# Early first gathers, a shorter first lag, and a combine in which TensorE adds two of four planes

## The reference, cut to what matters

```python
# first block, its last step
top_vals, top_idx = lax.top_k(logits, TOP_K)          # 4 of 32 experts for each token
weights = jax.nn.softmax(top_vals, axis=-1)
gu = xblk @ w_gu[e] + b_gu[e]                         # for the tokens of each expert
act = (up + 1.0) * gate * jax.nn.sigmoid(SWIGLU_ALPHA * gate)
y = act @ w_down[e] + b_down[e]                       # summed per token with weights
h = h + g2 * y
x = rmsnorm(h, final_norm_w)
# second block, its first step
h = rms_norm(x, norm_mix_pre[l])
proj = h @ w_in[l]
```

## Time and profile before

| | |
|---|---|
| median of 3 runs | 2189.33 us (2187.8 to 2194.87) |
| the profiled execution's own time | 2191.0 us |
| its span, first to last instruction | 2189.2 us |
| TensorE / VectorE / ScalarE / GpSimd busy | 1967.4 / 933.3 / 375.2 / 375.4 us |
| bytes moved, mean rate | 557.00 MB, 254 GB/s |
| mean granted TensorE clock | 0.948 |

### The profile page before, as it was taken

The page is one execution under the profiler, slowest core; times in us unless marked ns, Lnnn a source line. Parts: engine busy times, 40 slices in busy tenths (PEclk is TensorE's granted clock), DMA queues, the critical chain, the costliest instruction groups (busy, mean ns, idle before and its releaser), DMA issues. The chain is left out here.

```text
span 2189.2 us, 42428 instructions
## 1 busy us (share of the span) xinstructions
PE 1967.4 (90%) x17767; PEld 1045.4 (48%) x17767; DVE 933.3 (43%) x1774; ACT 375.2 (17%) x622; POOL 375.4 (17%) x428
## 2 busy tenths in 40 slices
PE   5889985999889999989899983799988999999998
PEld 3445552444234444434243431444776568885443
DVE  2552443333232333323233325365646465556564
ACT  2221230111111111111011101243233120000000
POOL 2930001222122222222122222100220000000000
PEclk9999997999899999999899996799998899999999
DMA  9433757999999999999999998210101402223441
GB/s 368 153 117 119 270 201 300 371 413 422 423 422 422 422 422 422 423 423 423 422 421 423 422 414 310 101 39 1 40 26 40 164 0 77 104 89 133 184 170 61
DMA packets 123668, 557.00 MB, mean 254 GB/s; under 512 B 16066, under 2 KB 19238, under 8 KB 74274
## 3 DMA queue, kind: packets, MB, share of 16 engines
q1 hardware_dynamic: 114272, 537.25, 61.3%
q0 software_dynamic: 8256, 16.83, 2.0%
q10 hardware_dynamic: 994, 0.71, 0.1%
HBM read 542.53 MB, written 16.92 MB: 256 GB/s over the span
## 5 line engine op out<-in xcount | busy, mean ns | idle before, releaser
L1427 PE MATMUL ps<-W,x_modulated 128*32 128x512 f32 x2640 | 321.1, 609 | 41.5 <-DMA W<-in_w_gu 31.0
L1547 DVE TENSOR_SCALAR gate<-ps 128x256 f32<-128x256 f32 x77 | 32.7, 425 | 541.4 <-PE ps L1431 541.4
L1427 PEld LDWEIGHTS ps<-W,x_modulated 128*32 128x32 f32 x2640 | 90.9, 111 | 224.5 <-issue 157.5
L1427 PE MATMUL ps<-W_high,x_modulated 128*32 128x512 f32 x1376 | 174.0, 613 | 17.3 <-DMA W_high<-in_w_gu 14.7
L1516 ACT ACTIVATE sig<-gate 128x256 f32<-128x256 f32 x81 | 33.8, 417 | 834.5 <-DVE gate L1547 789.5
L1443 PE MATMUL ps<-W,hidden_turned 128*32 128x256 f32 x2736 | 163.0, 381 | 0.0
L1940 PE MATMUL ps<-turned_rows,W 128*128 128x512 f32 x336 | 148.0, 599 | 2.6 <-PEq L132 2.3
L1443 PEld LDWEIGHTS ps<-W,hidden_turned 128*32 128x32 f32 x2736 | 101.4, 111 | 60.3 <-issue 17.1
L1367 POOL DMA_INDIRECT x_rows<-moe_xn,rows_idx x83 | 109.9, 1324 | 73.5 <-POOL rows_idx L1364 65.7
L2989 PE MATMUL ps<-turned_rows,W 128*128 128x256 f32 x512 | 116.4, 380 | 2.3 <-PE ps L2989 2.2
L1364 POOL COPY rows_idx<-slot_rows 128x1 int32 (+1 forms) x83 | 23.0, 277 | 554.9 <-DVE x_turned L1531 554.9
(11 more groups left out here) (591 smaller groups left out, 2794.7 us busy)
## 6 DMA issues: line engine op xcount, KB each, us to landing
W<-in_w_gu SPq DMA_DIRECT2D x139, 1024.0 KB
W<-in_w_down SPq DMA_DIRECT2D x71, 1024.0 KB
W_high<-in_w_gu SPq DMA_DIRECT2D x69, 1024.0 KB
W_high<-in_w_down SPq DMA_DIRECT2D x35, 1024.0 KB
W<-in_mlp_w SPq DMA_DIRECT2D x32, 1024.0 KB, 6.8
W<-in_w_ada SPq DMA_DIRECT2D x12, 2048.0 KB, 9.0
turned_rows<-in_w_gu SPq DMA_DIRECT2D x24, 1024.0 KB
h<-in_w_gu SPq DMA_DIRECT2D x24, 1024.0 KB
```

The costliest lines, as they stand in the source:

```text
L1427: last = pe.matmul(gu_out(j), xs[:, kk, :], quarter(ex.view(n), j), start=kk == 0, stop=False)
L1547: dve.tensor_scalar(gate[:], gu_bank[:, 0:256], SWIGLU_LIMIT, None, ALU.min).then_inc(gated, 1)
```

## The change

It has four parts.

1. In `phase_first` the last tile's residual and normed rows are stored by ScalarE's queue instead of SyncE's, right after they are made, with semaphores of their own (`h_last`, `xn_last`). Clearing `x_rows` moves into `phase_first`, and `y_rows` is cleared there too.
2. `phase_moe` begins with two gathers at once, sub-block 0 into `yb` and sub-block 1 into `xg`, with the row numbers read straight from `m.idx4`. `FIRST_LAG` goes from 5 to 2.
3. The two scatters of a pair share one copy of row numbers, and the second no longer waits for the first to have landed.
4. In the combine TensorE multiplies planes 0 and 1 of a tile with two diagonals of route weights into PSUM (`sums`). VectorE adds planes 2 and 3 as before, and then PSUM in two halves (`add_sums`). VectorE does the gain multiplication of every tile, ScalarE keeps every residual and makes the route diagonals, and GpSimd does nothing. The order of steps within each engine's stream is new.

The core of the diff:

```diff
-            store(3)
             sp.wait_ge(tr_x, 2 * TT)
-            for b in range(2):
-                sp.wait_ge(xm[b], 16 * TT // 2)
+            sp.wait_ge(xm[0], 32)
+            sp.wait_ge(xm[1], 16)
+            sp.wait_ge(xn_last, 16)
             ex.load(sp, 18)
...
             rooted(3)
+            act.dma_start(moe.h[tile(TT - 1), :], k.h[:, TT - 1, :]).then_inc(h_last, 16)
             keep_x(3)
             strip(3)
+            act.wait_ge(stripped, TT)
+            act.dma_start(moe.xn[(TT - 1) * 4 * P:TT * 4 * P, :].rearrange("(t q) c -> t (q c)", q=4), strips[:, (TT - 1) % 2].rearrange("p q k c -> p (q k c)")).then_inc(xn_last, 16)
...
-FIRST_LAG = 5
+FIRST_LAG = 2
...
+            def scatter_pair(u):
+                pool.wait_ge(y_out, u * 16 + 16)
+                pool.tensor_copy(to_idx[:], m.y_idx[:, bass.ds(u, 2)]).then_inc(to_set, 2)
+                for part, held in enumerate((yb[:], yb_2)):
+                    pool.wait_ge(to_set, u + 1)
+                    pool.wait_ge(y_ready, u + (part + 2))
+                    pool.sem_inc(scatters, 1)
+                    pool.indirect_dma_start(m.y, bass.IndirectOffsetOnAxis(ap=to_idx[:, part:part + 1], axis=0), held, None, bounds_check=NO_ROW - 1, oob_is_err=False).then_inc(y_out, 16)
+
+            gather(yb[:], m.idx4[:, 0:1], x_first)
+            gather(xg[:], m.idx4[:, 1:2], x_in)
             pool.dma_start(w_one[:], a["const_no_row"][0:1, 0:1]).then_inc(y_out, 16)
-            pool.wait_ge(xg_zero, 1)
-            gather(0)
...
         for i in range(TT):
-            for q in range(TOPK):
-                if i and q == 3:
-                    mean(i - 1)
+            for q in range(BY_PE, TOPK):
                 add(i, q)
-            if i and i < TT - 1:
+            if i:
+                mean(i - 1)
+            add_sums(i)
+            if i:
                 scales(i - 1)
+            gain(i)
...
+        def sums(i):
+            pe.wait_ge(self.routes, BY_PE * (i + 1))
+            for q in range(BY_PE):
+                pe.wait_ge(self.got[i][q], 16)
+            for s in range(2):
+                for q in range(BY_PE):
+                    last = pe.matmul(ps[2 * i + s][:], self.route[i % 3][:, q, :], self.rows[i][:, q, 512 * s:512 * s + 512], start=q == 0, stop=q == BY_PE - 1)
+                last.then_inc(self.summed, 1)
...
+        for i in range(TT):
+            sums(i)
+            if i:
+                turn(i - 1)
+        turn(TT - 1)
...
         for i in range(TT):
             squares(i)
+            if i == 0:
+                act.wait_ge(self.summed, 2)
+                route(3)
+            if i:
+                turned(i - 1, 0)
             roots(i)
-            if i < TT - 1:
-                turned(i)
+            if i:
+                turned(i - 1, 1)
+                keep(i - 1)
```

More of the change, by code:

```diff
@@ L1407, in _ @@
                 u = pool.snap(i)
-                next_gather(u + 2)
-                scatter(u)
-                scatter(u + 1, yb_2)
-                next_gather(u + 3)
-            combine.gpsimd(pool)
-            pool.wait_ge(x_in, end * 16 + 32)
+                next_gather(u, 2)
+                scatter_pair(u)
+                next_gather(u, 3)
+            pool.wait_ge(x_in, end * 16 + 16)
         @block.tensor
@@ L1521, in _ @@
                 sigmoid(act.snap(i))
+            act.wait_ge(hid_ready, end)
             combine.scalar(act)
@@ L1527, in _, with place_x @@
             wide = lambda i: k.modc[:, i, :, 0].rearrange("p (q o) -> p q o", o=1).to_broadcast([P, KD, SUB])
[L1529 to L1531 removed]
+            def place_x(u, rows=xs, landed=None, held=xg):
+                if landed is None:
+                    dve.wait_ge(x_in, u * 16)
+                else:
+                    dve.wait_ge(landed, 16)
+                dve.transpose(xt[:].rearrange("p q t -> p (q t)"), held[:]).then_inc(x_turn, 1)
                 dve.wait_ge(x_turn, u + 1)
@@ L1750, in roots, with turned, keep, route @@
             act.activation(root[:, i, :], root[:, i, :], ACT.Sqrt).then_inc(self.sd, 1)
-        def turned(i):
-            for s in range(2 if i < TT - 1 else 1):
-                act.wait_ge(self.tr, 2 * i + s + 1)
-                for kk in range(4 * s, 4 * s + 4):
-                    last = act.activation(hT[:, kk, tile(i)], ps[2 * i + s][:, tile(kk % 4)], ACT.Copy, scale=k.vec[:, VR + kk:VR + kk + 1])
-                last.then_inc(self.ev_a, 1)
+        def turned(i, s):
+            act.wait_ge(self.tr, 2 * i + s + 1)
+            for kk in range(4 * s, 4 * s + 4):
+                last = act.activation(hT[:, kk, tile(i)], ps[2 * i + s][:, tile(kk % 4)], ACT.Copy, scale=k.vec[:, VR + kk:VR + kk + 1])
+            last.then_inc(self.ev_a, 1)
+        def keep(i):
+            out, gained, scale = self.keep(i)
+            act.wait_ge(self.rec, i + 1)
+            act.activation(out, gained, ACT.Copy, scale=scale).then_inc(self.kept, 1)
+        def route(i):
+            for q in range(BY_PE):
+                act.activation(self.route[i % 3][:, q, :], k.ident[:], ACT.Copy, scale=self.m.weights[:, i, q:q + 1]).then_inc(self.routes, 1)
+        for i in range(3):
+            route(i)
         for i in range(TT):
             squares(i)
-            roots(i)
-            if i < TT - 1:
-                turned(i)
-        turned(TT - 1)
-        out, gained, scale = self.keep(TT - 1)
-        act.wait_ge(self.rec, TT)
-        act.activation(out, gained, ACT.Copy, scale=scale).then_inc(self.kept_a, 1)
-        act.wait_ge(self.kept_a, 1)
+            if i == 0:
[3 more added lines that the diff above has]
+                turned(i - 1, 0)
+            roots(i)
+            if i:
+                turned(i - 1, 1)
+                keep(i - 1)
+        turned(TT - 1, 0)
+        keep(TT - 1)
+        act.wait_ge(self.kept, TT)
         act.wait_ge(self.ev_a, 2 * TT - 1)
```

113 lines of the change are left out of this document (51 added, 62 removed).

## The result

The changed kernel took 2163.03 us in the median of four runs (2161.36 to 2164.13), the kernel before 2190.77 beside it (2187.8 to 2194.87). The ratio is 0.9871, with a 95% interval of 0.9853 to 0.989: 28.3 us less, 24 to 32. The forecast was 2169 us, some 20 us less.

A forecast was written before the change was run, and what follows sets the result against it. DMA was taken to bound the expert phase, TensorE its start, chains of small steps the combine. Front 5.85 us (4.1 + 1.75) plus 14.2 for scatter and combine made 20.1, median 2169; own range 2164 to 2175, overall 2163 to 2179.

The forecast's parts named there:

- Stores: End of the first phase: SyncE's last chunk issue ends at 337.15, 4.1 us earlier.
- the store lands no earlier: Rival, first phase: DMA engines have as many bytes ahead of the store; 4.1 us less gain, 2173; chance 0.08.
- Gathers: Start of the expert phase: the gather takes the small load's place, so first rows come 1.75 us earlier.
- Lag: Start of the expert phase: the shorter lag moves matmuls about and removes none; costed at nothing.
- Scatter: Before the combine: the second scatter starts sooner, first plane used 1.2 us earlier, bounds 0 and 2.8.
- The combine: Last copy at 1377.7 instead of 1391.94: gain 14.2 us, of which 1.2 is the scatter's; bounds 11.9 and 19.
- half-clock bound: Combine, TensorE bounding: 8.6 us a tile, end 1379.0; VectorE's bound 6.3 and 1374.4; the middle, 1376.7, was taken.
- The pacing rival: Combine: the in-order loop over VectorE, ScalarE and TensorE still paces at 11.5 us a tile; time 2177; chance 0.13.
- everything behind it shifted alike: Sign, after the combine: its last copy comes about 20 us earlier and all later work shifts equally.
- the stream only moves: Expert phase: the stream moves as much as TensorE's first matmul, so the front's 5.85 us count fully.
- the stream swallows the front: Rival, expert phase: DMA engines set the time from the first pair on, cutting the 5.85 us; 2175; chance 0.05.
- slower stream: Rival, expert phase: lower stream rate; 2.2% cancels everything, 3% gives 2196; chance 0.04, plus 0.04 for a smaller loss.

The follow-up runs named there:

- this part alone: Kernel before with only the early gathers and what goes with them, lag as before: 2187.54 us, ratio 0.9987.
- before_warm16: Kernel before with 16 small identity matmuls on TensorE ahead of the combine: 2189.01 us, ratio 0.9985.
- combine_only: Kernel before with only the combine changed (all of part 4): 2171.92 us, ratio 0.9918.
- after_lag5: Changed kernel with FIRST_LAG back at 5: 2161.11 us, ratio 0.985.
- lent work: Small identity matmuls added on TensorE ahead of the combine in the kernel before: 190, ratio 1.0044; 110, ratio 0.9982; 16, ratio 0.9985.
- sums_first_all512: Changed kernel with two tiles' sums ahead of the first turning and W, h, turned_rows, W_high starting on multiples of 512 bytes: 2155.21 us, ratio 0.9834.

## Why the prediction was right or wrong

The stores, the gathers and the scatters did what was told, the combine gained in part for other reasons, and the whole was too small: 20 us for 28. The median fell on the lower edge of the range, and beside the kernel before, the gain of 28.3 us lies past the 26 at which the range ended (2189 to 2163). (The chances at its end are added up wrongly too: by the rivals' own, faster had 0.92 and slower 0.04.)

**Stores: right.** 4.1 us were predicted at the barrier. It came 4.5 earlier in the means, 4.0 counted from the projection. In the profiled execution the last issue of the phase ended at 333.52 + 1.82 = 335.34 for the 337.15 forecast, because the row numbers, the gate as forecast, came 2.4 us earlier by chance; the three issues behind them took 2.3 us for 1.65. SyncE's wait for the store fell from 15.9 to 8.9 us: the normed rows landed 11.1 us after their issue (318.11 to 329.25) where it had been 16.9 (322.32 to 339.23). The rival that the store lands no earlier is thereby out, and with it the sentence of the Trainium skill behind it ("DMA: Bandwidth & Descriptors", section "Issuing engines are not separate DMA queues") when taken at its word for a single transfer behind a full queue.

**Gathers: right.** 1.75 us predicted, 1.6 measured in the means, 1.0 with this part alone. **Lag:** costed at nothing, it lost about 0.7 us. **Scatter: right**, 1.0 for 1.2.

**The combine: right in the profiled execution for partly wrong reasons, and under-sized in general.** Seam and combine gained 14.2 us there, and 14.2 were forecast, which is luck: two errors cancel. The sums of a tile were priced at four matmuls of 0.45 us, 1.8 us, from the 3.60 us for "x8" in the earlier trace rows. They take 3.60 at the full clock. The x in such a row counts records, and an fp32 matmul leaves two. In before_warm16, 16 matmuls read:

```profile
1329.80 3.84 PE L1503 MATMUL ps<-ident 128*128 128x128 f32 x32
```

So the pace is set through TensorE at either clock: 6.67 us a tile at the full one (2.05 + 3.60, then VectorE's last half-add and the scales), in which VectorE has to wait 0.77 us for the sums; and 9.4 us where the turning and part of the sums ran at half. The forecast had 6.3 and 8.6. With the true price its half-clock bound would have been 3.8 + 7.2 + 0.7 + 0.5 = 12.2 us a tile, slower than the old order. What made up for it is the clock, for which I had taken the middle between the two bounds: in combine_only and after_lag5 it was full from the sums of the first tile to the last turning, in the profiled execution it fell back for one turning and part of the sums behind it. Hence 38.4 and 38.3 us, or 41.7. Over the traces the combine gains 15.4 us for the 13.0 predicted. The pacing rival is out: no tile took 11.5.

**The step that failed: "everything behind it shifted alike", and its counterpart in front, that the stream only moves.** Two terms of the sum stood at nothing and were not: the length of the stream and what follows the combine.
- The stream lasts 3.5 us less, in every kernel in which the two buffers of the small rows start on a multiple of 256 bytes, and in no other with the old start of W. I had read the move of x_rows and y_rows as a way to clear them early. Of all that could change the rate of the saturated stretch I had considered only a loss, and held against it that nothing in the steady stretch is changed; the place of two of its buffers was.
- The tail is 4.1 us shorter in the means (798.9 for nine traces of the old combine without lent work, 794.8 for seven of the new). 2 of it are waits of TensorE 200 to 250 us behind the combine, which before_warm16 shows going without the change; by exclusion they depend on where the later instructions lie in its program. The rest goes with how long the clock stayed full in those 800 us (TensorE's busy time there is 760 to 767 us for the same work), and what decides that is open.

For the pair of profiled executions the account closes: 26.9 us for 20.1, of which the stream gave 3.3 and the tail 2.5, while the front gave 1.75 more than forecast (7.6 for 5.85, with 2.4 of chance in it) and lost 0.7 again. In the means 3.5 + 4.1 + 2.4 in the combine are more than the 8 that were missing; the means of single traces carry a microsecond or two of chance. The rivals "the stream swallows the front" and "slower stream" are out: from the first pair to the long issue nothing was lost but 0.7 us, and the stream ran faster.

## What to carry to other kernels

Where DMA engines bound a kernel, look at the start address of every buffer that they touch, the small ones too: an edit that only reorders allocations can move the time, and a test for it costs one pad. Before a matmul's price is taken from a grouped row, divide by the matmuls in the code and not by the count in the row. And a change that adds or removes instructions of an engine can shift waits hundreds of microseconds later; a few harmless instructions in the kernel before tell that apart from the change.

## What the runs showed of the hardware

- 1 KB rows that start 32, 96, 128 or 160 bytes behind a multiple of 256 cost the saturated stream 3.5 us over some 150 gathers and scatters of 128 rows. As an estimate that is 3.5 x 16 engines / (150 x 128) = 2.9 ns a row, and more if only one of the two buffers counts. For 8 KB rows in W it was 1.5 us over 186 chunks, 1.0 ns a row by the same reckoning.
- The Trainium skill ("DMA: Bandwidth & Descriptors", section "How a descriptor splits into AXI transactions") says that a transfer is cut into pieces that begin on 256-byte boundaries, and that one starting off such a boundary fetches from the boundary below it. The traces agree with the step at 256 bytes: start offsets 0 behind one gave 920.7 to 921.1 us, offsets 32, 96, 128 and 160 gave 924.2 to 924.7, and moving h, turned_rows and W_high from one multiple of 256 to another gave nothing. That it is the splitting which costs the time no run here shows.
- A store of 512 KB, issued from ScalarE's queue while SyncE's queue held seven chunks of 1 MB, landed after 11.1 us; from SyncE's own queue, behind the same chunks, after 16.9.
- In two traces of the same instructions TensorE's clock fell from full to half ahead of a turning in one (after a wait of 3.29 us, changed kernel) and held in the other (2.75 us, combine_only); in sums_first_all512 it held through 3.75 us. What decides it is open.
- An fp32 matmul leaves two records in the profile: 16 read x32, 110 read x220, 190 read x380.
- Identity matmuls of 128 columns in fp32, back to back, take 0.226 us each (24.83 us for 110, at a granted clock of 1.00).
